# A hybrid decoder step on one core: constants in two groups, another order at the end of the samples' stage, and the decays squared on VectorE

## The chip, the core and the metric

The kernel runs on one core of a Trainium2 chip. The time is that of one execution on the device, in microseconds; each figure is the median over several runs of the same program. The engines are called as in the profile: PE (TensorE, the matrix multiplier), DVE (VectorE), ACT (ScalarE), POOL (GpSimd) and SP (SyncE, which issues most transfers). Each engine takes its own instructions in order and waits for others by semaphores.

## What is computed

One inference step of a decoder trunk with two layers, for a prompt of 512 tokens and, beside it, 8 samples of 8 tokens each (576 tokens in all, width 1024, float32). Layer 0 has a gated delta rule (4 heads of 128, a causal convolution of width 4, decays per head) beside a causal pooling, behind one input and one output projection. Layer 1 has a recurrent block (RG-LRU). Each mixer and each mixture of experts (16 experts, two per token) is followed by a layer norm. Cut to what the change touches:

```python
def delta_pool_mixer(x, ...):
    proj = x @ w_in
    qkv, z, b_raw, a_raw, u = jnp.split(proj, [c0, c1, c2, c3], axis=-1)
    qkv, conv_new = causal_conv(qkv, conv_hist, conv_w)
    ...
    o, s_new = gated_delta_rule(q, k, v, g, beta, s0)
    o = o * lax.rsqrt(jnp.mean(o * o, -1, keepdims=True) + RMS_EPS) * norm_w
    o = o * jax.nn.silu(z).reshape(bsz, T, A_HEADS, A_DV)
    ...
    y = jnp.concatenate([o_a, o_b], axis=-1) @ w_out

def rglru_mixer(x, ...):
    ...
    log_a = -C_GATE * r * jax.nn.softplus(-lam)
    a = jnp.exp(log_a)
    bt = jnp.sqrt(-jnp.expm1(2.0 * log_a)) * gi * xc
    # h_t = a_t * h_(t-1) + bt_t, then (h * y_branch) @ w_out
```

## The kernel before

Everything is written out by hand, one function per engine; the order on each engine is the order of the code, and counting semaphores tie the engines together. SBUF is one large tile `work` with many views whose lives follow one another. Tokens come in five tiles: four of 128 rows (the prompt) and one of 64 (the samples).

**The start.** SP issues the input (`x_prompt`, then `x_sample`, semaphore `x_in`), the router's weights and bias, the small columns `wab_in` of the input projection, five small transfers of histories and parameters (`hist_in`), and then the weights of the input projection, 1 MB at a time, into four slots `W0` (`w_in`). POOL makes the constants (`constants`, from L2410): first a memset of every one, then selects (`keep_where`, L2404) that cut `ident` and the masks out of them, then a few counters; its last instruction, the cast to `inv_cnt` (L2457), signals `consts_ready`. After it POOL issues two tiny transfers (`gpar`, for the gates). PE waits for `x_in` and `consts_ready` and transposes the tiles (`to_channels`, L609, eight per tile, two tiles in flight); ACT rounds each (`XT_HIGH`, L1248) and DVE makes the rest (`XT_LOW`, L1696). PE transposes the histories (L894 to L900), DVE prepares `wab` (L1912 to L1919), and PE runs its first product with it (L907, L908) and then twenty column blocks of the projection (`project`, L622, L623). DVE's `gates` (L1724 to L1740) come behind PE's first product, and its twelve convolutions behind the gates. From the fourth block on PE adds up squares with the constant `sum_col`.

**The end of the samples' stage.** The delta rule goes over four prompt chunks and then the samples. At its end the state of each head h is updated: PE multiplies (`state_update(h)`, L855, into banks 2 and 3 for even h, 5 and 6 for odd), DVE adds to the state (`new_states(h)`, L1886, eight instructions). Meanwhile the RMS norm of the outputs is applied: PE spreads the roots of head h (`root_spread(h)`, L863 and L864, banks 4 and 7; from the second on it waits for `rmsb_out`, that is for DVE to have read the one before), DVE multiplies (`normed(h)`, L1893 and L1894), POOL multiplies by the gate Z (L2533, `mix_a`). In between PE does early parts of the output projection (`out_part`, L964); the rest follows the last spread and reads `WO_HEADS`, 2 MB that SP issues behind the last state product. SP stores the new states (2 MB) behind `new_states(3)`, and then loads the first experts' weights.

**The second mixer.** Eight units m of 128 channels, in two halves of four. PE computes two gates per unit (L1223, L1224), ACT their sigmoids, then per unit the exponential (`XT[m]`, L1660, `lru_a`) and the tangent (`R_[m]`, L1663, `lru_t`), then the four square roots (L1667, each behind `lru_w`). Between them the square of the exponential is needed: POOL makes it (`squared`, L2618, `lru_a2`), DVE uses it (`root_input`, L2338, `lru_w`). DVE's `recurrence` (L2345 to L2355) and `result` (L2360, `mix_a`) follow the root of their unit. PE's output projection (L1014) takes unit after unit.

Behind each mixer a layer norm, the router and a loop over 16 experts (L1067, L1094) follow.

## Time and profile before

| what | us |
|---|---|
| median of 3 runs | 1407.63 |
| lowest, highest | 1405.70, 1408.05 |
| the profiled execution | 1408.48 |
| its span in the trace | 1406.70 |
| PE busy in the span | 1244.5 (88%) |
| DVE, ACT, POOL busy | 968.3 (69%), 730.8 (52%), 183.6 (13%) |
| mean granted clock of PE | 0.935 |

The times of the trace count from the start of the span; the execution is 1.78 us longer than it. PE's granted clock is given as a share of full speed (2.4 GHz). A busy share is a mean over stages with different limits: what a wait costs is read from its stage.

### The profile page before, as it was taken

What the parts mean: (1) busy time and instruction counts of PE and PEld (TensorE: products, weight loads), DVE (VectorE), ACT (ScalarE), POOL (GpSimd) and SP (SyncE); (2) the same over time, 40 slices, a digit from 0 to 9 for tenths busy, and PEclk for the clock granted to TensorE, in tenths of its full rate; (3) what the DMA queues carried; (4) which work ended last, traced back from release to release, by engine and by line L of the source; (5) the groups of instructions that cost most, each with busy time, mean ns of one, the idle gap of its engine ahead of it and who ended that gap; (6) DMA issues with size and microseconds to landing.
All of it is one profiled execution on the core that took longest, in us unless ns stands there. A gap on an engine that the chain in (4) does not pass through costs nothing.

```text
span 1406.7 us, 18287 instructions
## 1 busy us (share of the span) xinstructions
PE 1244.5 (88%) x6605; PEld 1008.7 (72%) x6605; DVE 968.3 (69%) x1441; ACT 730.8 (52%) x1011; POOL 183.6 (13%) x251
## 2 busy tenths in 40 slices
PE   4999988889999699999999289998987999999970
PEld 3988887777445588888888189964456888888860
DVE  3766355441534599999997553738656999999957
ACT  2543242221101388888886553256133888888844
POOL 4011442200300010000000300031001100000002
PEclk9999999996899699999999599999987999999995
DMA  6211051001242689999994822030545899999835
GB/s 204 61 61 60 1 191 33 1 1 53 86 183 90 233 331 403 417 417 405 419 408 147 255 85 91 1 150 1 198 173 220 340 408 420 411 417 403 350 109 198
DMA packets 63102, 296.61 MB, mean 211 GB/s; under 512 B 6624, under 2 KB 32969, under 8 KB 50752
## 3 DMA queue, kind: packets, MB, share of 16 engines
q1 hardware_dynamic: 51136, 252.78, 46.6%
q0 software_dynamic: 7296, 26.22, 5.2%
q10 hardware_dynamic: 4608, 16.78, 3.0%
q8 instruction: 40, 0.66, 0.2%
q14 instruction: 22, 0.18, 0.0%
HBM read 268.87 MB, written 26.89 MB: 210 GB/s over the span
## 4 chain that ended last, share of the span: by engine, by line
PE 83%; DVE 9%; ACT 2%; issue 2%; POOL 2%; DMA 2%; POOLq 0%; DVEq 0%; ACTq 0%
PE bank L1067 24%; PE bank L1094 12%; PE bank L977 6%; PE bank L622 5%; PE bank L623 4%; PE bank L648 4%; PE bank L650 4%; PE bank L964 2%; PE bank L1014 2%; PE bank L1057 2%; PE bank L1223 2%; PE bank L988 2%; PE bank L609 1%; PE bank L718 1%; PE bank L1085 1%
## 5 line engine op out<-in xcount | busy, mean ns | idle before, releaser
L1248 ACT ACTIVATE GU_HIGH<-work 128x1024 fp32r<-128x1024 f32 x256 | 270.2, 1060 | 63.3 <-PE bank L1067 59.2
L1067 PE MATMUL bank<-GU_HIGH,XGT_HIGH 128*128 128x512 f32 x512 | 203.0, 397 | 6.1 <-DVE XGT_LOW_B L2206 6.1
L2012 DVE TENSOR_TENSOR WGT_LOW<-work,GU_HIGH 128x1024 fp32r<-128x1024 f32 x128 | 155.5, 1223 | 13.4 <-ACT GU_HIGH L1248 5.5
L1248 ACT ACTIVATE WDN_HIGH<-work 128x1024 fp32r<-128x1024 f32 x128 | 135.4, 1063 | 44.2 <-PE bank L1094 44.2
L2012 DVE TENSOR_TENSOR WUP_LOW<-work,GU_HIGH 128x1024 fp32r<-128x1024 f32 x128 | 153.1, 1222 | 7.3 <-ACT GU_HIGH L1248 3.1
L2228 DVE TENSOR_TENSOR WDN_LOW<-work,WDN_HIGH 128x1024 fp32r<-128x1024 f32 x128 | 151.7, 1221 | 7.6 <-ACT WDN_HIGH L1248 3.7
L1067 PEld LDWEIGHTS bank<-GU_HIGH,XGT_HIGH 128*128 128x128 f32 x512 | 96.9, 189 | 26.0 <-DVE XGT_LOW_B L2206 6.9
L1248 ACT ACTIVATE work<-bank 128x512 f32<-128x512 f32 (+5 forms) x124 | 53.4, 469 | 115.1 <-PE bank L711 26.9
L1248 ACT ACTIVATE W_HIGH<-work 128x1024 fp32r<-128x1024 f32 x36 | 37.8, 1058 | 129.6 <-PE bank L623 80.0
L1067 PE MATMUL bank<-GU_HIGH,XGT_LOW_A 128*128 128x512 f32 x256 | 100.6, 393 | 0.0
L1067 PE MATMUL bank<-WGT_LOW,XGT_HIGH 128*128 128x512 f32 x256 | 100.2, 391 | 0.0
L1067 PE MATMUL bank<-GU_HIGH,XGT_LOW_B 128*128 128x512 f32 x256 | 100.0, 391 | 0.0
L1067 PE MATMUL bank<-WUP_LOW,XGT_HIGH 128*128 128x512 f32 x256 | 99.9, 390 | 0.0
L1094 PE MATMUL bank<-WDN_HIGH,HT_HIGH 128*128 128x512 f32 x240 | 96.4, 402 | 0.0
L1094 PE MATMUL bank<-WDN_HIGH,HT_LOW 128*128 128x512 f32 x240 | 93.7, 390 | 0.0
L1094 PE MATMUL bank<-WDN_LOW,HT_HIGH 128*128 128x512 f32 x240 | 93.5, 390 | 0.0
L977 PE MATMUL bank<-work,XT 128*128 128x512 f32 (+1 forms) x192 | 83.2, 593 | 0.0
L1463 ACT ACTIVATE lnw<-lnw 128x1 f32<-128x1 f32 (+1 forms) x10 | 2.0, 203 | 138.2 <-DVE lnw L2034 138.2
L977 PEld LDWEIGHTS bank<-work,XT 128*128 128x128 f32 (+1 forms) x192 | 32.8, 172 | 48.6 <-issue 48.0
L2558 POOL COPY idx_cur<-idx_all 128x1 int32 x28 | 7.0, 251 | 395.6 <-PE bank L1057 395.6
L1757 DVE SCALAR_TENSOR_TENSOR work<-work,par 128x512 f32<-128x512 f32 x120 | 56.9, 517 | 2.1
L1931 DVE TENSOR_TENSOR W_LOW<-work,W_HIGH 128x1024 fp32r<-128x1024 f32 x20 | 25.2, 1262 | 46.8 <-ACT W_HIGH L1248 46.6
(479 smaller groups left out, 2903.9 us busy)
## 6 DMA issues: line engine op xcount, KB each, us to landing
work<-in_moe_w_gate_dram SPq DMA_DIRECT2D x32, 2048.0 KB, 10.7
work<-in_moe_w_up_dram SPq DMA_DIRECT2D x32, 2048.0 KB, 10.5
work<-in_moe_w_down_dram SPq DMA_DIRECT2D x32, 2048.0 KB, 9.7
y_rows<-work ACTq DMA_DIRECT2D x32, 512.0 KB
work<-in_ab_w_in_dram SPq DMA_DIRECT2D x10, 1024.0 KB, 5.5
work<-in_c_w_in_dram SPq DMA_DIRECT2D x8, 1024.0 KB, 5.9
x_rows<-X SPq DMA_DIRECT2D x8, 512.0 KB, 2.6
work<-in_c_w_out_dram SPq DMA_DIRECT2D x1, 4096.0 KB, 15.7
```

Of the source, the lines that this page charges most:

```text
L622: mm(bank[c % 2][:, 0:TH], w[:, k, :], x[:, k, 0:TH], **ends)
L623: last = mm(bank[(3, 6)[c % 2]][:, 0:TH], w[:, k, :], x[:, k, TH:T], **ends)
L648: last = mm(bank[c % 3][:, 0:TH], w[:, k, :], x[:, k, 0:TH], **ends)
L650: last = mm(bank[(3, 6, 7)[c % 3]][:, 0:TH + 2], w[:, k, :], x[:, k, TH:T + 2], **ends)
L964: last = mm(bank[2 * (t % 2) + half][0:ROWS[t], :], XT[:, k, tile_cols(t)], (WO_A, WO_B)[l][k][:, 512 * half:512 * half + 512], start=(k = ...
L977: last = mm(bank[2 * (t % 2) + half][0:ROWS[t], :], XT[:, k, tile_cols(t)], (WO_A, WO_B)[l][k][:, 512 * half:512 * half + 512], start=(k = ...
L1067: last = mm(psum, x, w, start=(k == m == 0), stop=(k == KD - 1 and m == 2))
L1094: last = mm(bank[banks[half]][:, :], x[:, f, :], w[:, f, cols], start=(f == n == 0), stop=(f == 3 and n == 2))
L1248: return nc.scalar.activation(out, in_, ACT.Copy, scale=scale)
L1757: last = V.scalar_tensor_tensor(dst, src, w, dst, ALU.mult, ALU.add)
L2012: V.tensor_tensor(low[u][:, 2 * n:2 * n + 2, :], w[u][:, 2 * n:2 * n + 2, :], high, ALU.subtract)\
L2228: V.tensor_tensor(WDN_LOW[u][:, f, :], WDN[u][:, f, :], WDN_HIGH[:, f, :].bitcast(F32), ALU.subtract).then_inc(down_split, 1)
```

## The change

There are three parts. (1) At the start, POOL makes `ident` first and signals it by itself (`ident_ready`); then the constants and cleared buffers that are used early, signalled by `consts_ready`; then it issues the `gpar` transfers, and then makes the masks, signalled by `masks_ready`. PE's first transposes wait for `ident_ready`; DVE waits for `masks_ready` behind its gates, PE ahead of its first sum of squares. SP issues the first weights `W0[0]` ahead of the histories and the router's weights behind all weights of the projection. (2) At the end of the samples' stage, PE's `root_spread(2)` goes ahead of `state_update(3)`, and DVE's `new_states(3)` behind the last `normed`. (3) In the second mixer, DVE squares the decays inside `root_input`, and POOL's `squared` is gone.

```diff
--- before.py
+++ after.py
@@ -299,7 +299,7 @@
         state_out, y_out = sem("state_out"), sem("y_out")
         xrows_out, holds_ready, idx_ps, idx_ready = sem("xrows_out"), sem("holds_ready"), sem("idx_ps"), sem("idx_ready")
 
-        consts_ready = sem("consts_ready")
+        ident_ready, consts_ready, masks_ready = sem("ident_ready"), sem("consts_ready"), sem("masks_ready")
         xt_ps, xt_lo, xt_hi = sem("xt_ps"), sem("xt_lo"), sem("xt_hi")
         hist_ps, hist_out, ab_ps, rows_ready = sem("hist_ps"), sem("hist_out"), sem("ab_ps"), sem("rows_ready")
         wab_ready, gate_act, gate_dve = sem("wab_ready"), sem("gate_act"), sem("gate_dve")
@@ -520,10 +520,9 @@
                 sp.dma_start(to[0:TS, 4, :], x_sample.rearrange("s l d -> (s l) d")).then_inc(x_in, 16)
 
             load_x(X_IN)
-            sp.dma_start(rw[:, :, :], router_w.rearrange("(k p) e -> p k e", p=P)).then_inc(router_in, 16)
-            sp.dma_start(rbias[:, :], router_bias.partition_broadcast(P)).then_inc(router_in, 16)
             win = ab_w_in[0].rearrange("(k p) c -> p k c", p=P)
             sp.dma_start(wab_in, win[:, :, 2048:2056]).then_inc(wab_sem, 16)
+            sp.dma_start(W0[0], win[:, :, 0:256]).then_inc(w_in[0], 16)
             sp.dma_start(chist_rows[0:24, :], state_delta_conv[0].rearrange("s j c -> (s j) c")).then_inc(hist_in, 16)
             sp.dma_start(phist_rows[0:120, :], state_pool[0].rearrange("s j c -> (s j) c")).then_inc(hist_in, 16)
             sp.dma_start(par_rows[0:48, :], a_conv_w[0].rearrange("j (c p) -> (j c) p", p=P)).then_inc(hist_in, 16)
@@ -534,12 +533,15 @@
             for n, c in enumerate(cols):
                 if n >= 4:
                     sp.wait_ge(proj_ps, 2 * (n - 4) + 2)
-                sp.dma_start(W0[n % 4], win[:, :, c:c + 256]).then_inc(w_in[n % 4], 16)
+                if n:
+                    sp.dma_start(W0[n % 4], win[:, :, c:c + 256]).then_inc(w_in[n % 4], 16)
                 if n == 3:
                     sp.wait_ge(consts_ready, 1)
                     for l in range(2):
                         sp.dma_start(slot_list[l].rearrange("(p n) o -> p (n o)", p=P), zero_i[:, :])\
                           .then_inc(lists_zeroed, 16)
+            sp.dma_start(rw[:, :, :], router_w.rearrange("(k p) e -> p k e", p=P)).then_inc(router_in, 16)
+            sp.dma_start(rbias[:, :], router_bias.partition_broadcast(P)).then_inc(router_in, 16)
             sp.wait_ge(proj_ps, NPROJ)
             load_x(X)
             lnp(0, 0, ln_mix_g, ln_mix_b)
@@ -598,7 +600,7 @@
                         pe.wait_ge(norm_scaled if n == 2 else norm_done, (n - 1) * NT + t + 1)
                     elif t == 0:
                         pe.wait_ge(x_in, 32)
-                        pe.wait_ge(consts_ready, 1)
+                        pe.wait_ge(ident_ready, 1)
                     if n == 3 and t == 0:
                         pe.wait_ge(st1_out, 2)
                     if n * NT + t >= 2:
@@ -883,8 +885,8 @@
                 state_update(2)
                 root_spread(1)
                 out_part(0, 0, (NH + 3,), False, False)
+                root_spread(2)
                 state_update(3)
-                root_spread(2)
                 root_spread(3)
 
             def mixer0():
@@ -914,6 +916,7 @@
                         n = c - 3
                         pe.wait_ge(sq_done, n + 1)
                         if n == 0:
+                            pe.wait_ge(masks_ready, 1)
                             pe.wait_ge(rows_ready, 1)
                         ends = dict(start=(n == 0), stop=(n == 7))
                         mm(bank[4][0:8, :], sum_col[:, n, :], SQ[:, n % 2, 0:TP], **ends)
@@ -1903,9 +1906,9 @@
                 normed(0)
                 new_states(2)
                 normed(1)
-                new_states(3)
                 normed(2)
                 normed(3)
+                new_states(3)
 
             def mixer0():
                 dve.wait_ge(consts_ready, 1)
@@ -1948,6 +1951,7 @@
                 split_w(0)
                 split_w(1)
                 gates()
+                dve.wait_ge(masks_ready, 1)
                 dve.wait_ge(hist_out, 3)
                 for c in range(NCHUNK):
                     split_w(c + 2)
@@ -2333,8 +2337,10 @@
                         dve.wait_ge(ext1_zeroed, 1)
                     conv(m, EXT1[m % 3], lhistT[:, m, :], XC[:, m, :], KD, par[:, 32 + m:33 + m]).then_inc(conv_done, 1)
                 def root_input(m):
+                    dve.wait_ge(lru_a, m + 1)
+                    mine(V.tensor_tensor(TMP[:, m % 2, :], XT[:, m, :], XT[:, m, :], ALU.mult))
                     dve.wait_ge(lru_t, m + 1)
-                    dve.wait_ge(lru_a2, m + 1)
+                    mine.settle()
                     V.scalar_tensor_tensor(R_[:, m, :], TMP[:, m % 2, :], 1.0, R_[:, m, :], ALU.add, ALU.mult)\
                         .then_inc(lru_w, 1)
 
@@ -2405,23 +2411,32 @@
                                    channel_multiplier=mult))
 
             def constants():
-                for m, v in ((ident, 0.0), (ones, 1.0), (m_strict_bd, -1.0), (m_strict_off, -1.0), (m_strict_s, -1.0),
-                             (m_incl, 1.0), (m_incl_s, 1.0), (m_before, 1.0), (own_sample, 1.0), (ms_col, 0.0),
-                             (m_lower4, 1.0), (sel_gc, 0.0), (sel_row, 0.0), (sum_col, 0.0), (COL, 0.0), (scores, 0.5)):
+                do(G.memset(ident[:], 0.0))
+                G.affine_select(out=ident[:, :], in_=ident[:, :], compare_op=ALU.not_equal, fill=1.0, base=0,
+                                pattern=[[-1, P]], channel_multiplier=1).then_inc(ident_ready, 1)
+                mine(G.memset(wab, 0.0))
+                for m, v in ((ones, 1.0), (COL, 0.0), (scores, 0.5)):
                     mine(G.memset(m[:], v))
                 mine(G.memset(zero_i[:, :], 0))
                 mine(G.memset(norm_eps[:, 0:1], LN_EPS / ALPHA ** 2))
                 mine(G.memset(RT, 0.0))
                 mine(G.memset(keep, 1.0))
-                mine(G.memset(wab, 0.0))
                 mine(G.memset(U[:, :, 0:HIST], 0.0))
                 for buf in EXTB:
                     mine(G.memset(buf[:, 0:CONV - 1], 0.0))
+                do(G.iota(iota_i[:, :], pattern=[[1, 16]], base=1, channel_multiplier=0))
+                do(G.tensor_copy(inv_cnt[:, :], iota_i[:, :]))
+                mine(G.memset(keep[:, 0:TP].rearrange("p (c l) -> p c l", l=P)[:, :, 0], 0.0))
+                do(G.memset(keep[:, TP:T].rearrange("p (c l) -> p c l", l=LS)[:, :, 0], 0.0))
                 do(G.iota(tok_id[:, :], pattern=[[P, NT]], base=0, channel_multiplier=1))
-                mine(G.memset(keep[:, 0:TP].rearrange("p (c l) -> p c l", l=P)[:, :, 0], 0.0))
-                mine(G.memset(keep[:, TP:T].rearrange("p (c l) -> p c l", l=LS)[:, :, 0], 0.0))
-                keep_where(ident[:, :], [[-1, P]], 0, 1, 1.0, ALU.not_equal)
-
+                G.tensor_copy(tok_f[:, :], tok_id[:, :]).then_inc(consts_ready, 1)
+                for n, src in enumerate((a_dt_bias, a_log_decay)):
+                    pool.dma_start(gpar[32:36, n:n + 1], src.rearrange("o h -> h o")).then_inc(gates_in, 16)
+                for m, v in ((m_strict_bd, -1.0), (m_strict_off, -1.0), (m_strict_s, -1.0),
+                             (m_incl, 1.0), (m_incl_s, 1.0), (m_before, 1.0), (own_sample, 1.0), (ms_col, 0.0),
+                             (m_lower4, 1.0), (sel_gc, 0.0), (sel_row, 0.0), (sum_col, 0.0)):
+                    mine(G.memset(m[:], v))
+                mine.settle()
                 keep_where(m_strict_bd[:, :], [[-1, P]], -1, 1)
                 keep_where(m_strict_bd[:, :].rearrange("p (b c) -> p b c", b=2), [[-64, 2], [0, 64]], 0, 1)
                 keep_where(m_strict_bd[:, :].rearrange("p (b c) -> p b c", b=2), [[64, 2], [0, 64]], 63, -1)
@@ -2445,16 +2460,13 @@
                 keep_where(ms_col[:, :, :], [[1, NH], [-1, NH]], 0, 0, 1.0 / P, ALU.not_equal)
                 keep_where(m_lower4[:, :, :], [[1, 4], [-1, 4]], -1, 0)
                 keep_where(sum_col[:, :, :], [[1, 8], [-1, 8]], 0, 0, 1.0, ALU.not_equal)
-                do(G.tensor_copy(tok_f[:, :], tok_id[:, :]))
                 do(G.iota(slot_no[:, :].bitcast(I32), pattern=[[1, P]], base=0, channel_multiplier=0))
                 do(G.tensor_copy(slot_no[:, :], slot_no[:, :].bitcast(I32)))
                 do(G.iota(iota_i[:, :], pattern=[[1, NE]], base=0, channel_multiplier=0))
                 do(G.tensor_copy(iota16[:, :], iota_i[:, :]))
-                do(G.iota(iota_i[:, :], pattern=[[1, 16]], base=1, channel_multiplier=0))
                 mine(G.tensor_copy(before16[:, :], m_before[:, :]))
-                mine(G.tensor_copy(ones16[:, :], ones[:, :]))
                 mine.settle()
-                G.tensor_copy(inv_cnt[:, :], iota_i[:, :]).then_inc(consts_ready, 1)
+                G.tensor_copy(ones16[:, :], ones[:, :]).then_inc(masks_ready, 1)
 
             def tail(ready, n, buf, to, c, done):
 
@@ -2489,8 +2501,6 @@
                 st.end(G.tensor_tensor(to, QKV[:, 0:4, cols], egB[:, :, 0:n], ALU.mult), i, "qd")
 
             def mixer0():
-                for n, src in enumerate((a_dt_bias, a_log_decay)):
-                    pool.dma_start(gpar[32:36, n:n + 1], src.rearrange("o h -> h o")).then_inc(gates_in, 16)
                 for c in range(NCHUNK):
                     tail(proj_out, c + 1, EXTB[c % 3], tails, c, tail_done)
                 pool.wait_ge(conv_done, NCHUNK)
@@ -2611,19 +2621,9 @@
                     pool.wait_ge(lru_gates_done, 2 * m + 2)
                     G.tensor_tensor(GI[:, m, :], GI[:, m, :], XC[:, m, :], ALU.mult).then_inc(lru_x, 1)
 
-                def squared(m):
-                    pool.wait_ge(lru_a, m + 1)
-                    if m >= 2:
-                        pool.wait_ge(lru_w, m - 1)
-                    G.tensor_tensor(TMP[:, m % 2, :], XT[:, m, :], XT[:, m, :], ALU.mult).then_inc(lru_a2, 1)
-
                 half = KD // 2
                 for m in range(half):
                     gated_input(m)
-                for m in range(half):
-                    squared(m)
-                for m in range(half):
-                    squared(half + m)
 
             constants()
             mixer0()
```

What the order of the instructions becomes, at three places. On PE at the end of the samples' stage, from the third part of the early output projection (L964) on; L855 is a state update, L863 and L864 a spread. Before:

```order
L964 MATMUL bank<-work,XT 128x512 x2
L855 MATMUL bank<-work 128x512 x2
L863 MATMUL bank<-work,sel_row 128x512
L864 MATMUL bank<-work,sel_row 128x64
L863 MATMUL bank<-work,sel_row 128x512
L864 MATMUL bank<-work,sel_row 128x64
L964 MATMUL bank<-work,XT 128x512 x24
```

Now (the lines have moved by two or three):

```order
L967 MATMUL bank<-work,XT 128x512 x2
L865 MATMUL bank<-work,sel_row 128x512
L866 MATMUL bank<-work,sel_row 128x64
L857 MATMUL bank<-work 128x512 x2
L865 MATMUL bank<-work,sel_row 128x512
L866 MATMUL bank<-work,sel_row 128x64
L967 MATMUL bank<-work,XT 128x512 x24
```

The last state update has moved from ahead of the two last spreads to between them. On DVE at the same place, from the second `normed` (the pair that writes XT) on; the eight instructions with `egl` are a state update. Before:

```order
L1893 SCALAR_TENSOR_TENSOR XT<-work,par,bank 128x512
L1894 SCALAR_TENSOR_TENSOR XT<-work,par,bank 128x64
L1886 SCALAR_TENSOR_TENSOR work<-work,egl,bank 128x128 x8
L1893 SCALAR_TENSOR_TENSOR XT<-work,par,bank 128x512
L1894 SCALAR_TENSOR_TENSOR XT<-work,par,bank 128x64
L1893 SCALAR_TENSOR_TENSOR XT<-work,par,bank 128x512
L1894 SCALAR_TENSOR_TENSOR XT<-work,par,bank 128x64
L2025 SCALAR_TENSOR_TENSOR X<-X,bank 128x512 x2
```

Now:

```order
L1896 SCALAR_TENSOR_TENSOR XT<-work,par,bank 128x512
L1897 SCALAR_TENSOR_TENSOR XT<-work,par,bank 128x64
L1896 SCALAR_TENSOR_TENSOR XT<-work,par,bank 128x512
L1897 SCALAR_TENSOR_TENSOR XT<-work,par,bank 128x64
L1896 SCALAR_TENSOR_TENSOR XT<-work,par,bank 128x512
L1897 SCALAR_TENSOR_TENSOR XT<-work,par,bank 128x64
L1889 SCALAR_TENSOR_TENSOR work<-work,egl,bank 128x128 x8
L2029 SCALAR_TENSOR_TENSOR X<-X,bank 128x512 x2
```

The last state update has moved behind the three `normed`. On POOL at the start, the first instructions now; the twelve masks, their selects and the counters follow behind the last row:

```order
L2414 MEMSET ident 128x128
L2415 ISA
L2415 AFFINE_SELECT ident<-ident 128x128
L2417 MEMSET work 128x544
L2419 MEMSET ones 128x128
...
L2427 IOTA iota_i 128x16
L2428 CAST inv_cnt<-iota_i 128x16
...
L2432 CAST tok_f<-tok_id 128x5
L2434 DMA gpar<-in_a_dt_bias_dram 4x1
L2434 DMA gpar<-in_a_log_decay_dram 4x1
L2438 MEMSET m_strict_bd 128x128
```

Before, the select of `ident` stood behind all memsets, and the transfers of `gpar` behind all constants.

## Rows read from the trace of the kernel before

**Rows 1.** The page, part 4: the chain that ended last, by line.
```profile
PE bank L1067 24%; PE bank L1094 12%; PE bank L977 6%; PE bank L622 5%; PE bank L623 4%; PE bank L648 4%; PE bank L650 4%; PE bank L964 2%; PE bank L1014 2%; PE bank L1057 2%; PE bank L1223 2%; PE bank L988 2%; PE bank L609 1%; PE bank L718 1%; PE bank L1085 1%
```

**Rows 2.** Waits of PE, 0 to 60 us: total, times, longest.
```profile
PE bank L609 <- POOL inv_cnt L2457: 16.3, 1, 16.3
```

**Rows 3.** Timeline of POOL, 0 to 45 us: start, length, line, work.
```profile
5.69 0.29 POOL L2404 TENSOR_SCALAR_AFFINE_SELECT ident<-ident 128x128 f32<-128x128 f32 x1
...
20.08 0.55 POOL L2493 DMA_DIRECT2D gpar<-in_a_log_decay_dram  x1
```

**Rows 4.** Timeline of SP's queue, 0 to 60 us: its DMA issues.
```profile
0.82 0.47 SPq L519 DMA_DIRECT2D work<-in_x_prompt_dram  x1
1.35 0.58 SPq L520 DMA_DIRECT2D work<-in_x_sample_dram  x1
...
12.04 5.70 SPq L537 DMA_DIRECT2D work<-in_ab_w_in_dram  x4
```

**Rows 5.** DMA issues, 0 to 40 us: count, KB each, median us to landing.
```profile
work<-in_x_prompt_dram SPq DMA_DIRECT2D x1, 2048.0 KB, 8.9
work<-in_x_sample_dram SPq DMA_DIRECT2D x1, 256.0 KB, 9.9
```

**Rows 6.** The chain that ended last, 15 to 31 us: start, length, work.
```profile
16.31 3.55 PE bank L609 x16
...
21.07 1.30 DVE XT_LOW L1696 x2
...
22.42 1.11 PE bank L609 x8
...
28.41 0.48 PE bank L907
```

**Rows 7.** Timeline of DVE, 0 to 70 us: the last instruction of the gates.
```profile
46.62 0.82 DVE L1740 TENSOR_TENSOR work<-work 4x512 f32<-4x512 f32 x2
```

**Rows 8.** Windows: span, PE, PEld, DVE, ACT, POOL busy, PE clock, DMA, GB/s.
```profile
18.00:20.00 2.00, 1.85 (x10) 1.55 (x8) 0.52 (x1) 1.20 (x3) 0.70 (x1) 1.00 1.10 351
...
30.00:32.00 2.00, 2.00 (x10) 1.93 (x9) 1.58 (x2) 0.00 (x0) 0.00 (x0) 0.50 0.03 8
```

**Rows 9.** The chain that ended last, 362 to 392 us.
```profile
374.41 1.93 PE bank L855 x4
...
376.36 2.15 DVE work L1886 x8
378.51 0.66 DVE XT L1893
...
379.42 2.07 PE bank L863 x2
...
381.81 1.08 issue
```

**Rows 10.** Windows, columns as in rows 8, around 380 us.
```profile
376.00:378.00 2.00, 1.54 (x5) 0.66 (x4) 1.64 (x7) 0.00 (x0) 0.00 (x0) 1.00 0.15 27
...
387.00:388.00 1.00, 1.00 (x2) 0.34 (x1) 0.00 (x0) 0.00 (x0) 0.00 (x0) 0.50 1.15 349
```

**Rows 11.** Timeline of DVE in the second mixer (brackets: idle before).
```profile
950.53 0.75 DVE L2345 TENSOR_TENSOR work<-work 128x576 f32<-128x576 f32 x1
...
969.58 0.76 DVE L2338 SCALAR_TENSOR_TENSOR work<-work 128x576 f32<-128x576 f32 x1 [2.54 <-POOL work L2618]
```

**Rows 12.** Timelines of ACT and of POOL in the second mixer.
```profile
949.80 2.40 ACT L1667 ACTIVATE work<-work 128x576 f32<-128x576 f32 x4
...
948.22 1.53 POOL L2618 TENSOR_TENSOR work<-XT 128x576 f32<-128x576 f32 x1 [0.75 <-DVE work L2338]
```

**Rows 13.** Timelines of PE and of DVE at the second mixer's end.
```profile
990.62 3.60 PE L1014 MATMUL bank<-work,XT 128*128 128x512 f32 x8
...
988.59 0.76 DVE L2360 TENSOR_TENSOR XT<-work 128x576 f32<-128x576 f32 x1
```

**Rows 14.** DMA issues, 370 to 400 us, columns as in rows 5.
```profile
work<-in_ab_w_out_dram SPq DMA_DIRECT2D x1, 2048.0 KB, 8.6
```

## The prediction, made before the change was run

> **What bounds the kernel now.** I read the chain of work that ended last first: it lies mostly on TensorE (PE), and the two expert loops alone (L1067, L1094) are 36% of the span [rows 1]. The change touches neither loop. So it can only move the time at which PE gets through the stages around them, and I asked of each of its three places: does PE, or the chain that feeds it, wait there?
>
> At the start it does. PE has one long wait, 16.3 us, for `inv_cnt`, the last constant that POOL makes [rows 2]. `ident`, the only constant that the first transposes read, is ready at 5.98 and is made behind the memsets of all the others [rows 3]. The other thing that PE waits for is the input: `x_prompt` is issued at 0.82 and lands 8.9 us later, at 9.7; `x_sample` is issued at 1.35 and lands 9.9 us later, at 11.25 [rows 4, 5]. Behind the wait the chain goes tile by tile over PE, ACT and DVE, and PE starts its long run at 28.41 [rows 6].
>
> At the end of the samples' stage it does too. The chain goes from PE's state update (L855) to 2.15 us of DVE's state update (L1886), to DVE's `normed` (L1893), to PE's spread (L863, L864) [rows 9]. PE was through with the spread before at about 377.5 (376.34, and half of the 2.39 us, 379.42 to 381.81, that the same two lines take later at half clock) and starts the next at 379.42: 1.9 us of waiting for a `normed` of under 1 us that stands behind eight state instructions. The granted clock is 0.5 (1.2 GHz) from this pause on and still at 388; before it, it was 1.00 [rows 10].
>
> In the second mixer it does not. DVE waits for POOL's squares, 2.54 us in one place, yet its first recurrence (L2345, at 950.53) needs ACT's first square root, which starts at 949.80 and takes about 0.7 us [rows 11, 12]. The out-projection (L1014) has its last eight matmuls at 990.62, while DVE's last product ended at 989.35 [rows 13].
>
> **The start (-4.3 us).** `ident` becomes POOL's first work, a memset and 0.29 us of select, so ready before 2. PE then waits for `x_sample` alone and starts at 11.3 instead of 16.3: -5.0. The bounds: it cannot start before `x_prompt` is there, at 9.7 (-6.6). On the other side 1 MB of weights (`W0[0]`) now stands behind it in SP's queue where 72 KB of router weights stood; if the two shared the engines instead of following each other, 1 MB at the 351 GB/s of the weight stretch [rows 8] would cost 3.0 us (-2.0). I take -5.0, since `x_sample` stays second in the queue.
>
> PE gives a part back. The first sixteen transposes took 3.55 us (222 ns each), the eight of a later tile 1.11 (139 ns) [rows 6]: PE begins slow after its long idling. Tiles 2 and 3 may now come while it is still slow: 2 x 8 x 0.083 = 1.3 us. A tile starts only when DVE's 1.30 us for an earlier one are over (21.07 to 22.37, then PE at 22.42 [rows 6]), so part of it falls into PE's pauses. Bounds 0 and 1.3; I take half, 0.7. The granted clock reads 1.00 over these slow transposes [rows 8]; by that column there would be no such term, and the start would bring -5.0. The Trainium skill (TensorE: Matmul & The Clock Gate, What's actually happening) says that the default state is throttled and that activity releases it. That rule would hold the 0.7. The 222 ns speak against the column, and for them I keep the term. The long run began at 0.50 [rows 8]; I take the same again.
>
> What moves beside it. SP's queue: the first 1 MB of the four issued from 12.04 on [rows 4] goes ahead of the five small histories, the router weights (72 KB in two issues) behind all ten. PE reads the histories right behind the last tile, near 20.5; they were all issued by 12.0, and the 3.0 us of one more megabyte before them leaves 5 us. Bounds: 0, and 1 us if they land as late as `x_sample` did after its issue (12.0 + 9.9 = 21.9, less the pauses). I take 0. `W0[0]` itself is wanted by ACT near 21.5 and is now issued about 9 us sooner. POOL: `consts_ready` falls near 5; the two `gpar` transfers take the 4.5 us that they took (16.17 to 20.63), and and the masks take their part of the stretch from 5.98 to 16.17, 9.5 us, and 2 us of memsets [rows 2, 3]: they end near 21. DVE waits for `masks_ready` behind its gates, whose last instruction ended at 47.44 [rows 7] and now ends near 43: cost 0. Queued behind that wait are DVE's convolutions, and on PE the first sum of squares.
>
> **The samples' stage (-2.5 us).** From the end of the out-projection part at 374.41 PE now does: spread(2) 1.2, state update 1.93, spread(3) 1.2, then waits 1.08 for the last `normed`, as before [rows 9]. That ends at 379.8 instead of 382.89: -3.0. DVE has `normed(2)` during PE's state update, so spread(3) waits for nothing. The 3.0 are the 1.9 of waiting, and the 1.2 that the last spread took longer at half clock. But now 4.3 us of narrow products and the 1.08 pause stand in a row, and I expect the clock to fall there again, with a spread or the state update slowed. Bounds: the clock stays up and the 5.2 us at half clock from 382.9 to past 388 are saved too, -2.6; or it falls at once and stays low as long again, +2.6. I take 0.5 back.
>
> What is late next. The 2 MB `WO_HEADS` waits for the last state product, which comes 1.2 us later: issued at 377.6, landed 8.6 us later [rows 14] at 386.2. PE has the early part first, sixteen records at 3.60 us for eight [rows 13], so wants it at 387.0 at the soonest. Cost 0, with 0.8 us to spare. The state store goes out 3.5 us later and SP's first expert weights behind it; the loops that use them are 100 us away. DVE's moved 2.15 us lie where it waits for the out-projection.
>
> **The second mixer (0).** DVE takes over eight squares of 0.75 us (its product of this size [rows 11]). Per unit it needs 0.75 + 0.76 = 1.51 us, and ACT starts its roots at 949.80 in any case, behind its own table load. DVE begins when the first exponential is there, so its fourth root input ends near 949.3 and the recurrences begin with ACT's first root as now. What goes is DVE's idling. Were all of the squares to come on top, it would be 3.0 us per half, less 1.3 us of slack in the second [rows 13]; DVE idles 2.54 us ahead of its second half, so I take neither.
>
> **Sum.** -4.3 - 2.5 + 0 = -6.8 us. The profiled execution took 1408.48 us (1.78 around its span of 1406.70), which gives 1401.7. It is 0.85 above the median of the runs, 1407.63; against that, 1400.8 us.
>
> **The rivals.**
> *More comes of it* (chance 0.10): the clock does not fall in the samples' stage, or `x` lands by 10. Then -2.6 or -1.3 more: 1398.2 for the first. Against it: narrow products and a pause remain.
> *One term fails* (0.20): `x_sample` lands by 14.3 beside `W0[0]`, or the slow clock takes the samples' gain back. The sum is -3.8 to -4.3: 1403.6.
> *POOL stands in DVE's way* (0.06): the masks are now made while DVE splits the tiles. If they end 1.5 us later than 21, DVE's `WAB` instructions meet POOL's last ones (selects and casts, 0.29 us as the row of `ident` [rows 3]), and waiting for two of them costs 0.6 us on the path: 1401.4. The nearest row is a square on POOL beside DVE's work, 1.53 us [rows 12]. The Trainium skill (SBUF — State Buffer, Who interferes with whom) states an exclusive lock between these two engines, the later one waiting for the whole instruction.
> *The new wait decides* (0.03), the case on the other side: `masks_ready`. It costs one for one from the moment that the masks are later than DVE's gates, near 43; past 49.9 it has eaten the 6.8, and at 52 the time is 1409.7. For it: all convolutions and PE's fourth projection hang on it. Against: the 11.5 us of mask work would have to take 3.5 times as long.
> That the squares' move does nothing is part of the forecast itself.
>
> **How the numbers follow.** The forecast, both terms within a microsecond or so, has 0.61. About 0.2% (2.8 us) is what a measurement of this kernel can tell from no change; faster then means below 1404.8. The forecast, the first and the third rival lie there, and of the second three quarters: 0.61 + 0.10 + 0.06 + 0.15 = 0.92, of which I move 0.03 to "same" for terms that I have not seen: 0.89. Same 0.08, slower 0.03. The range takes in the first two rivals and what the runs themselves scatter (1405.7 to 1408.05): 1397.5 to 1404.5.
>
> **What would show it.** PE's first transpose at 11.3, released by the transfer and no longer by POOL; tiles 2 and 3 at 139 to 222 ns a transpose; the long run from 24.1 instead of 28.41; DVE never waiting for `masks_ready`. Then spread(3) without a wait, `WO_HEADS` not waited for. In the second mixer DVE's waits for POOL gone, and the distance from ACT's first root to PE's L1014 unchanged. Wrong would be: a later landing of `x_sample`, a wait on the histories at L894, or squares that show up in the chain.

## The result, and the profile after

The changed kernel takes 1398.51 us, the median of 4 runs (1397.54 to 1400.39), against 1407.84 us for the kernel before, run beside it (4 runs, 1405.70 to 1410.73). The ratio is 0.9935 with a 95% interval of 0.9914 to 0.9957, that is -9.2 us, between -12.1 and -6.1. It is faster, as forecast. The predicted 1400.8 us lies 2.3 us above the measured time, and the predicted gain of 6.8 us lies inside the interval, near its small end. The profiled execution took 1398.68 us with a span of 1396.3, so 2.4 us lie outside the span, where it was 1.8 before. Three executions in the experiments below took 1520, 1622 and 4796 us, one of them of the kernel before, and are left out of the ratios.

First the chain that ended last in the changed kernel, from 0 to 25 us (start, length, work), against [rows 6]:

```profile
1.35 9.68 DMA work<-in_x_sample_dram
...
11.07 1.98 PE bank L611 x8
...
15.61 3.69 PE bank L611 x16
...
24.12 0.48 PE bank L909
```

POOL is gone from it. PE's first transpose is released by the transfer of `x_sample`, as predicted: 11.07 instead of 16.31, so 5.24 us sooner. The long run (L909, L907 before) starts at 24.12 instead of 28.41, so 4.29 us sooner. The 0.95 us between the two numbers is what PE gave back in this profile: tiles 2 and 3 took 3.69 us for sixteen transposes, 230 ns each, where the kernel before had such a tile in 1.11 us. It is not the same in every profile, as the experiments show.

Next POOL's and SP's timelines of the changed kernel, against [rows 3, 4]:

```profile
4.95 0.75 POOL L2434 DMA_DIRECT2D gpar<-in_a_dt_bias_dram  x1
5.72 0.54 POOL L2434 DMA_DIRECT2D gpar<-in_a_log_decay_dram  x1
6.24 0.23 POOL L2438 MEMSET m_strict_bd<- 128x128 f32 x1
...
17.41 0.29 POOL L2469 CAST ones<-ones 128x128 f16<-128x128 f32 x1
```

```profile
1.98 0.57 SPq L524 DMA_DIRECT2D work<-in_ab_w_in_dram  x1
2.59 2.88 SPq L525 DMA_DIRECT2D work<-in_ab_w_in_dram  x1
5.52 4.66 SPq L526 DMA_DIRECT2D work<-in_state_delta_conv_dram  x1
...
11.71 5.22 SPq L537 DMA_DIRECT2D work<-in_ab_w_in_dram  x3
```

The masks are ready at 17.70, sooner than the 21 that I expected. They and their memsets take 11.5 us as estimated (6.24 to 17.70), but the two `gpar` issues take 1.3 us, not 4.5. PE's list of waits has no entry for the masks, and none for the histories. On SP's queue the issue of `W0[0]` (1 MB) holds the queue for 2.88 us and the next one for 4.66 us.

Then the end of the samples' stage in the chain of the changed kernel, against [rows 9]:

```profile
368.76 1.09 PE bank L865 x2
369.85 0.17 PE bank L866 x2
370.02 1.91 PE bank L857 x4
371.93 1.05 PE bank L865 x2
372.98 0.17 PE bank L866 x2
373.15 1.08 issue
374.23 22.54 PE bank L967 x48
396.76 3.43 PE bank L980 x8
```

DVE has left the chain. From the end of the early product to the output projection it is 5.47 us (368.76 to 374.23), where it was 8.48 (374.41 to 382.89): 3.01 us less, the predicted 3.0. The clock, windows of the changed kernel with the columns of [rows 8]:

```profile
375.00:377.00 2.00, 2.00 (x4) 0.97 (x3) 1.20 (x5) 0.00 (x0) 0.61 (x1) 0.50 1.02 418
387.00:388.00 1.00, 1.00 (x3) 0.38 (x2) 0.00 (x0) 0.00 (x0) 0.00 (x0) 1.00 0.93 197
```

It falls here again, as expected, but it comes back much sooner. Added up over windows of 1 us, it is at 0.50 for 3.4 us, from 374 to 378, where before it was at 0.50 for 10.2 us, from 378 to 389 [rows 10]. The L967 part (L964 before) runs without a pause, so `WO_HEADS` isn't waited for, and ends at 396.76 instead of 406.39: the gain has grown from 8.66 us at the projection's first product to 9.63, another 0.97 us. From the end of the early product to the end of this part it is 28.0 us instead of 32.0.

Last the second mixer, timelines of ACT, DVE and PE in the changed kernel (in brackets the idle time before), against [rows 11 to 13]:

```profile
939.67 2.40 ACT L1670 ACTIVATE work<-work 128x576 f32<-128x576 f32 x4
...
940.38 0.76 DVE L2351 TENSOR_TENSOR work<-work 128x576 f32<-128x576 f32 x1 [0.99 <-ACT work L1670]
...
958.04 0.76 DVE L2341 TENSOR_TENSOR work<-XT 128x576 f32<-128x576 f32 x1 [1.14 <-ACT XT L1663]
...
965.26 0.76 DVE L2351 TENSOR_TENSOR work<-work 128x576 f32<-128x576 f32 x1 [1.00 <-ACT work L1670]
...
956.24 24.20 PE L1017 MATMUL bank<-work,XT 128*128 128x512 f32 x56
```

DVE no longer waits for POOL. It waits for ACT, some 1 us in each half. From ACT's first root to the first record of the out-projection it is 16.57 us; before, the timelines have 949.80 and 966.48 for the two, 16.68 us. In this stage the squares' move is worth nothing, as predicted.

The spans differ by 10.4 us, the two executions by 9.8 (1408.48 and 1398.68), since 0.6 us more lie outside the span. The places above give 4.29 at the start, 3.01 in the samples' stage and 0.97 in the output projection, 8.3 together; the rest comes and goes on the way. Between the start and the samples' stage, where no wait that the change adds is felt, the gain grows from 4.29 to 5.65 us (374.41 against 368.76). It stands at 9.63 us behind the first output projection, at 7.96 at the last product of the first expert loop (773.14 against 765.18), at 10.24 at the second mixer's out-projection. What differs is the clock: added up over windows of 1 us as far as 1340 us, near the end of the last expert loop, PE's granted clock is at 0.50 for 143.4 us before and for 136.5 us after (over the whole spans 182.5 and 176.0). Half of the 6.9 us, up to 3.4, is what that can be worth. As many as 6.8 us of these 6.9 are what the samples' stage and its output projection differ by (10.2 against 3.4 us), which is where the change acts; elsewhere the two kernels gain and lose about as much.

### The profile page after: what moved, and what is told of

It is laid out like the page before. It is cut to its first block, busy times and chain, and to the rows that moved or that the text cites. A ratio compares the mean times of both kernels' runs of the same rounds, so it can differ in the third digit from the quotient of the medians.

```text
span 1396.3 us, 18281 instructions
## 1 busy us (share of the span) xinstructions
PE 1243.7 (89%) x6605; PEld 1009.9 (72%) x6605; DVE 972.4 (70%) x1449; ACT 730.6 (52%) x1011; POOL 172.2 (12%) x243
## 4 chain that ended last, share of the span: by engine, by line
PE 83%; DVE 9%; ACT 3%; issue 2%; DMA 2%; SPq 0%; POOL 0%; POOLq 0%; DVEq 0%; ACTq 0%
PE bank L1070 25%; PE bank L1097 13%; PE bank L980 6%; PE bank L624 5%; PE bank L625 4%; PE bank L650 4%; PE bank L652 4%; PE bank L967 2%; PE bank L1017 2%; PE bank L1060 2%; PE bank L1226 2%; PE bank L991 2%; PE bank L611 1%; PE bank L720 1%; PE bank L1088 1%
## 5 line engine op out<-in xcount | busy, mean ns | idle before, releaser
L1070 PEld LDWEIGHTS bank<-GU_HIGH,XGT_LOW_A 128*128 128x128 f32 x256 | 48.9, 191 | 10.5
## 6 DMA issues: line engine op xcount, KB each, us to landing
work<-in_moe_w_gate_dram SPq DMA_DIRECT2D x32, 2048.0 KB, 10.4
work<-in_moe_w_up_dram SPq DMA_DIRECT2D x32, 2048.0 KB, 10.2
y_rows<-work ACTq DMA_DIRECT2D x32, 512.0 KB, 10.4
```

The lines of the kernel that those rows point to most:

```text
L1070: last = mm(psum, x, w, start=(k == m == 0), stop=(k == KD - 1 and m == 2))
```

## The experiments

Ratios are to the kernel before, run on the same chip in the same set; microseconds are the ratio times its median of 1407.

**The parts alone.** Four kernels. `e1_start` and `e3_squares` are the change's hunks for the start and for the second mixer alone. `e2_samples` and `e4_dve_order` are

```diff
on DVE, e2_samples and e4_dve_order:
-                new_states(3)
                 normed(2)
                 normed(3)
+                new_states(3)
on PE, e2_samples alone:
+                root_spread(2)
                 state_update(3)
-                root_spread(2)
                 root_spread(3)
```

> Part 1 alone: the split constants, their order on POOL and the order of SP's first DMAs; the samples' stage and the second mixer as in the kernel before. Theory A (the three parts add up as the prediction priced them, and what the full change gained beyond 6.8 us is PE's clock, which falls elsewhere when the same work lies elsewhere): the first transpose at 11.1 instead of 16.3, the long run of matmuls of L907 from 24.1 instead of 28.4, and that 4.3 us kept to the end but for the clock: -4.3 us, from -7.7 to -0.9 if one more or one fewer stretch of 3.4 us is at 1.2 GHz at the end. Theory B (the start itself earns more later than its 4.3 us, for instance because the first mixer's transfers or DVE run further ahead): -7 us or more, with stalls that are gone in places other than the start, at an unchanged granted clock. If A holds, the difference of the spans minus half of the difference of the time at 1.2 GHz is the same 4.3 us plus what the stages' own waits differ.

> Part 2 alone: in the samples' stage PE's spread of the root of head group 2 ahead of the state update of 3, and DVE's new_states(3) behind the two normed steps; the rest as in the kernel before. Theory A: from the last L964 product of the stage to the first product of the output projection the stretch is 3.0 us shorter, as in the full change (from 8.5 to 5.5 us), and the total goes by -3.0, from -6.4 to +0.4 with a stretch of 3.4 us at 1.2 GHz more or fewer. Theory B (the reordering earns only when the earlier start comes with it): under 1.5 us gained at this place.

> Part 3 alone: DVE squares the decays of the second mixer itself. Theory A (DVE waited for ACT's roots anyway, and the four squares of a half, 3.0 us of DVE's time, go into that wait): 0, within 1 us, and from ACT's first root to the first product of the output projection 16.7 to 16.9 us as before. Theory B (POOL's squares stood in the way, since POOL and DVE share a port or since DVE's wait for two engines came through late): -1 to -2.5 us, seen between the same two points. Theory C (DVE becomes the one that is late): +1 to +3 us, seen there too.

> Only DVE's half of part 2: new_states(3) behind normed(2) and normed(3), with PE's order as before (state_update(3), then root_spread(2) and (3)). Theory A (what ended the stage late was DVE, which normed the last two groups behind a new_states that nobody there needed: L1886 took 2.15 us in the chain): most of the 3.0 us, -2.0 to -3.0, comes from DVE's half alone. Theory B (the halves need each other, since the spread of group 2 waited behind state_update(3) on PE, 1.93 us of L855 in the chain): at most -1.1 at this place, as one half takes away only its own part of the chain and the other takes its place.

| kernel | ratio, 95% interval | us |
|---|---|---|
| start alone | 0.9956 [0.9939, 0.9972] | -6.2 |
| samples' stage alone | 0.9976 [0.9960, 0.9993] | -3.4 |
| squares alone | 0.9995 [0.9981, 1.0008] | -0.7 |
| DVE's half of the samples' stage | 0.9998 [0.9980, 1.0016] | -0.3 |

The three parts add up to -10.3 us against the -9.2 of the whole. Within the intervals, which are some 2 us to either side for each, none needs another. The intervals of the start (-8.6 to -3.9) and of the samples' stage (-5.6 to -1.0) hold the 4.3 and the 2.0 to 3.0 that the traces show at their places. Nothing in the runs asks for theory B at the start: the long run begins at 24.19, as in the whole change. The squares alone give 16.74 us from ACT's first root to the first record of the out-projection (948.67 to 965.41), as theory A had it, and 44.33 us to the projection's second block (993.00), against 44.26 before (949.80 to 994.06). They also show which part the 0.6 us outside the span come with: 2.4 us lie outside it with the squares on DVE, 1.7 to 1.8 in the kernel before, in `e1_start` and in `e2_samples`. Why is open, the more so as `e6_twice`, which has squares on DVE too, has 2.0.

The samples' stage needs the clock of its spread told apart from its order. Kernel `e1_start` has the old order there. Its chain:

```profile
369.07 1.92 PE bank L857 x4
...
371.02 2.16 DVE work L1889 x8
373.18 0.66 DVE XT L1896
...
374.08 1.12 PE bank L865 x2
...
375.44 1.08 issue
376.52 23.55 PE bank L967 x48
```

It is the chain of [rows 9] link by link, except that the spread (L865 here, L863 there) takes 1.12 us and not 2.07, since the clock falls a little later. The stretch is 7.45 us (369.07 to 376.52). `e2_samples`, with both halves of the new order and the old start, takes 5.46 us (371.36 to 376.82), as theory A had it. So as far as the output projection, and with the spread near full speed, the reordering is worth 7.45 - 5.47 = 1.98 us, and the other 1.03 of the 3.01 are that spread's clock.

With DVE's half alone the stretch was 6.53 us (374.53 to 381.06), 0.92 less than 7.45; expected were at least 2.0 (theory A) or at most 1.1 (theory B). So B holds as far as the output projection. To the end of the projection it is another matter, as the table below shows.

**PE's half alone, the whole once more, the old queue, and the start given back.**

```diff
 after_again: the changed kernel, unaltered
 e9_pe_order (kernel before): root_spread(2) ahead of state_update(3); DVE's order as before
 e5_old_queue (start alone): SP issues rw, rbias ahead of wab_in, W0[0] behind the histories
 e8_masks_gate (changed kernel):
-                        pe.wait_ge(ident_ready, 1)
+                        pe.wait_ge(masks_ready, 1)
```

> The changed kernel once more, unaltered. Theory A (the parts earn 4.3 us at the start and 2.0 to 3.0 in the samples' stage, which is what the same points of the traces show at equal clock, and the rest of what was measured is where TensorE's time at 1.2 GHz happens to fall): the ratio comes out between 0.9935 and 0.9960, -5.6 to -9.2 us, and the profile again differs from the sum of the parts by half of the difference of the time at 1.2 GHz. Theory B (something lasting beyond the parts): again 0.9935 or below.

> Only PE's half of part 2: root_spread(2) ahead of state_update(3), DVE's order as before; the complement of the run with DVE's half, which took 6.53 us from the end of the last early L964 product to the output projection, where the kernel before took 8.48 (of this 0.95 because L863 ran at 1.2 GHz) and both halves take 5.46. Theory A (the halves split the 2.0 us evenly, each in its own link of the chain: PE's half hides the 1.93 us of state_update(3) under DVE's norm): 6.5 us, and the total by -1.0 but for the clock. Theory B (PE's half alone gives nothing, since DVE's norm of group 3 still ends last behind new_states): 7.5 us, no gain at this place.

> Part 1 without its change of SP's queue: the split constants as in the change, but SP issues the router's weights behind the input and the first block of the first mixer's weights behind the histories, as before; parts 2 and 3 left out. It is to be compared with part 1 alone, -6.2 us, and tells whether the queue's new order matters. Theory A (the clock of the start is the input's landing and ident alone): the first transpose at 11.1, the long run of L907 from 24.1, W0 of block 0 landed by 22 and nobody waiting for it; the time as part 1 alone within the scatter. Theory B (the queue's order carries part of the gain): PE waits for w_in behind the gate's columns, the first mixer's first matmuls start later by as much, up to 3 us.

> The changed kernel, but its first transpose waits for the masks (the end of all of POOL's constants, at 17.7 us) instead of for ident; the rest unaltered. It gives the start back and keeps all other moves. Theory A (each microsecond of the first transpose is one of the end): the first transpose at 17.7 instead of 11.1, the end later by 6.6 us than the changed kernel's, -1.5 to -4 us against the kernel before. Theory B (the start is worth less than it looks, since later stages wait for transfers or other engines that don't move with it): later by less than 4 us. Theory C (more than it looks): later by 8 us or more.

| kernel | ratio, 95% interval | us |
|---|---|---|
| the changed kernel again | 0.9948 [0.9932, 0.9965] | -7.3 |
| PE's half of the samples' stage | 1.0002 [0.9990, 1.0014] | +0.3 |
| start alone, old queue | 0.9964 [0.9950, 0.9978] | -5.1 |
| changed, first transpose behind the masks | 0.9997 [0.9985, 1.0009] | -0.4 |

The whole change came to -7.3 us this time, in the middle of what theory A gave. The -6.8 of the sum lies in both intervals, so the times alone show nothing lasting beyond the priced parts, and don't exclude 2 or 3 us of it. Its profile has the first transpose at 10.58, tiles 2 and 3 at full speed and the long run from 22.75, and again 28.0 us from the end of the early product to the end of the L967 part.

With PE's half alone, the chain from the same point on (374.22, the end of the early product):

```profile
374.22 1.09 PE bank L863 x2
...
375.47 1.93 PE bank L855 x4
...
377.42 2.16 DVE work L1886 x8
379.58 0.66 DVE XT L1893
...
380.48 2.07 PE bank L863 x2
...
382.87 1.08 issue
383.95 22.31 PE bank L964 x48
```

It is 9.73 us, 1.25 longer than the 8.48 before at the same clock (both have the spread at 2.07). That is worse than either theory had it (6.5 and 7.5 us, or a microsecond more with the slow spread). DVE still does its state instructions first, and these now wait for a state update that comes behind the spread. So neither half gives the 1.98: DVE's alone gains 0.92, PE's alone loses 1.25. The total of `e9_pe_order` shows no gain either.

The count up to the output projection leaves out what the clock does behind it. Measured from the same point, the end of the early product, in all profiles (us; the last column adds up windows of 1 us as far as the projection's part L964 or L967 goes):

| order | to the output projection | to the end of its part | clock at 0.50 |
|---|---|---|---|
| old, the kernel before | 8.48 | 32.0 | 10.2 |
| old, `e1_start`, `e3_squares`, `e5_old_queue` | 7.40 to 7.63 | 31.0 each | 6.8 each |
| PE's half alone | 9.73 | 32.0 | 6.8 |
| DVE's half alone | 6.53 | 28.8 | 3.4 |
| both halves, six profiles | 5.46 to 5.47 | 28.0 each | 3.4 each |

The six are the changed kernel twice, `e2_samples`, `e8_masks_gate`, and `e6_twice` and `e10_first_tile` from further below. So the shorter time at 1.2 GHz comes with the new order each time, whatever the start did: the stage is worth 3.0 us against three profiles of the old order and 4.0 against the kernel before's. Counted this way, DVE's half alone gives 2.2 of the 3.0, theory A's share after all, while its total (-0.3, from -2.8 to +2.3) can't tell.

The old queue gives the start's gain as well. W0[0] is then issued at SP's usual place behind the histories, the first transpose comes at 10.49, and PE waits for no weights. The two intervals overlap largely: the new order of the queue is worth nothing that can be measured. What does differ is the pace of the tiles, PE's timeline of this kernel:

```profile
10.49 3.33 PE L609 MATMUL bank<-ident,work 128*128 128x128 f32 x16 [10.49 <-DMA work<-in_x_sample_dram]
15.04 1.09 PE L609 MATMUL bank<-ident,work 128*128 128x128 f32 x8 [1.22 <-DVE XT_LOW L1697]
16.38 1.09 PE L609 MATMUL bank<-ident,work 128*128 128x128 f32 x8 [0.25 <-DVE XT_LOW L1697]
```

Tiles 2 and 3 are at full speed here, and the long run begins at 22.62, though the transposes began only 0.58 us sooner than in the changed kernel. It isn't the queue that does it: the changed kernel's second profile has the same. Nor is it the change. `e2_samples` and `e4_dve_order` have the old start, instruction for instruction, and their transposes begin at the same 16.23. Tile 2 in the second profile of the changed kernel, in `e2_samples`, and tiles 2 and 3 in `e4_dve_order`:

```profile
15.12 1.09 PE L611 MATMUL bank<-ident,work 128*128 128x128 f32 x8 [0.87 <-DVE XT_LOW L1699]
...
20.75 1.09 PE L609 MATMUL bank<-ident,work 128*128 128x128 f32 x8 [1.21 <-DVE XT_LOW L1696]
...
20.75 3.67 PE L609 MATMUL bank<-ident,work 128*128 128x128 f32 x16 [0.87 <-DVE XT_LOW L1696]
```

From the first transpose to the long run it is 12.1 us in the kernel before, in `e2_samples`, here, and 12.2 in the changed kernel's second profile; it is 13.0 to 13.4 in `e3_squares`, `e4_dve_order` and `e9_pe_order`, which have the old start, as in the changed kernel's first profile and `e1_start`. So the term that I took as half of 1.3 us is scatter of both kernels, not a price of the change. The long run begins at 28.33 to 29.61 in five profiles with the old start, and at 22.62 to 24.19 in six with the new one (without the two whose input is split and the one that waits for the masks).

Waiting for the masks moves the first transpose to 17.85 and the long run to 31.23, 7.1 us later than in the changed kernel, and costs 0.9997 - 0.9948, 6.9 us at the end, give or take some 3 us by the two intervals. At the end of the L967 part it is 7.3 us (404.11 against 396.76), so as far as there each microsecond of the start is kept; the end agrees with that (theory A) but wouldn't exclude 8. Against the kernel before, A's -1.5 to -4 us was missed: it is -0.4 (-2.1 to +1.3). The long run is 2.8 us later than before's, which eats up the 3 to 4 us of the samples' stage. It also shows what the split itself is for: with one semaphore for all constants in this order of POOL's, 17.7 us would still stand where 11.07 does.

**What is left to gain, and how much cover the squares have.** Four variants of the changed kernel; the last has both edits.

```diff
 e6_twice: each square of root_input(m) issued twice
 e7_no_pause, in out_and_route(0):
-                    pe.wait_ge(rmsb_out, NH)
                     e_dve.wait(pe, 0, "s2")
 e10_first_tile, on SP and on PE:
+            sp.dma_start(X_IN[:, 0, :], x_prompt[0, 0:P, :]).then_inc(x_first, 16)
+            sp.dma_start(X_IN[:, 1:4, :], x_prompt[0, P:4 * P, :]...).then_inc(x_in, 16)
...
                     elif t == 0:
+                        pe.wait_ge(x_first, 16)
                         pe.wait_ge(ident_ready, 1)
+                    elif t == 1:
                         pe.wait_ge(x_in, 32)
```

> The changed kernel with each of DVE's eight squares in the second mixer done twice: 8 x 0.75 = 6.0 us more on DVE between ACT's roots and the output projection, 3.0 in each half. Theory A (the four squares of a half are hidden, since DVE waits 1.0 to 1.1 us for ACT in each half and once between them, and PE has 1.45 us left behind DVE's last product; so about 4.5 us of cover is left beyond what the change used): from ACT's first root to the first product of the output projection 18.0 to 19.5 us instead of 16.7, the total +1.5, up to +3. Theory B (DVE is far from the end here): 16.7, +0. Theory C (the single squares were at the edge already): +6, the stretch 22 to 23.

> The changed kernel without PE's wait for rmsb_out in front of the early part of the output projection's second tile; PE then waits there for e_dve and, ahead of the late part, for mix_a. What ended the pause of 1.08 us in the changed kernel is not named in its chain. Theory A (it is this wait, that is DVE's L1896 and L1897 on head group 3): the pause goes, the out-projection begins behind L866, and the total goes by -1.1. Theory B (DVE's other products, for which e_dve waits, or the late part's wait for mix_a end as late as that): the pause stays or comes back 32 products of L967 on, total 0.

> The changed kernel, but the first 128 rows of the prompt come by a DMA and a semaphore of their own (0.5 MB), and PE's first eight transposes wait for these alone; the others wait for the other rows and the sample. Theory A (what bounds the start now is the landing of 2.25 MB, 9.7 us behind its issue, and after it a pace of 4.5 us per tile): the first transpose at 5 to 7 us, the second tile's at 10.0 to 11.5, the long run of L909 from 19.5 to 20.5 instead of 24.1, the total by -4. Theory B (the next thing is late: W0 of block 0 or wab, issued behind the input, or the histories): PE waits for w_in or wab_ready, the run begins at 21 or later and the total goes by -1 to -3. Theory C (the tiles' pace is lost where it is gained, since PE waits for the second tile): the run begins at 23 or later, total 0 to -1.

> The two edits together: the first tile by its own DMA, and no wait for rmsb_out ahead of the early part. Theory A: they add, -4 and -1.1: about -5 us against the changed kernel, -12 to -14 against the one before. Theory B (one of them gives nothing): as the better one alone.

| kernel | ratio, 95% interval | us |
|---|---|---|
| squares twice | 0.9960 [0.9942, 0.9978] | -5.6 |
| no pause | 0.9937 [0.9916, 0.9957] | -8.9 |
| first tile by itself | 0.9923 [0.9899, 0.9948] | -10.8 |
| both edits | 0.9914 [0.9888, 0.9940] | -12.1 |

Squares twice, timelines of ACT and PE:

```profile
939.02 1.83 ACT L1670 ACTIVATE work<-work 128x576 f32<-128x576 f32 x3
941.95 0.68 ACT L1670 ACTIVATE work<-work 128x576 f32<-128x576 f32 x1 [1.10 <-DVE work L2346]
...
957.94 13.90 PE L1017 MATMUL bank<-work,XT 128*128 128x512 f32 x32
972.63 10.57 PE L1017 MATMUL bank<-work,XT 128*128 128x512 f32 x24 [0.79 <-DVE XT L2368]
```

Root to out-projection is 18.92 us instead of 16.57, inside theory A's 18.0 to 19.5, and now ACT's fourth root waits for DVE, and PE for DVE's product. To the second block of the projection it is 47.57 us (to 986.59) against 44.15 (to 983.82), 3.4 us for 6.0 us of added work, about a microsecond of which is the clock. So some 2.6 to 3.6 us of the added work were still covered, less than the 4.5 that I expected; the single squares of the change are not at the edge. The total, 1.7 us above the changed kernel's -7.3, is near theory A's +1.5 too.

Without the wait for `rmsb_out` the chain has no pause:

```profile
376.62 1.53 PE bank L865 x2
378.16 0.32 PE bank L866 x2
378.48 23.50 PE bank L967 x48
```

The 1.08 us are gone at their place, so that wait was what ended them. But they aren't gained. The spread now takes 1.53 us instead of 1.05, and the part behind it 23.50 instead of 22.54: the clock falls before the spread is over and is at 0.50 for 6.8 us instead of 3.4. From the end of the early product to the end of the part it is 28.5 us (373.46 to 401.98), 0.5 longer than the 28.0 with the pause. In the total the kernel is at -8.9 against -7.3 and -9.2 of the changed kernel, which can't tell either way.

The first tile by itself, PE's timeline:

```profile
4.47 1.97 PE L615 MATMUL bank<-ident,work 128*128 128x128 f32 x8 [4.47 <-DMA work<-in_x_prompt_dram]
10.42 3.67 PE L615 MATMUL bank<-ident,work 128*128 128x128 f32 x16 [3.98 <-DMA work<-in_x_sample_dram]
14.95 1.09 PE L615 MATMUL bank<-ident,work 128*128 128x128 f32 x8 [0.86 <-DVE XT_LOW L1703]
```

The first 0.5 MB lands 3.6 us after its issue, and the long run begins at 20.88 instead of 24.12, 3.2 us sooner: between the 4 of theory A and the 1 to 3 of B. A took the first tile to save its whole pace of 4.5 us. But the second tile can't start before the rest of the input is there, so PE stands idle 3.98 us between them. No wait for weights is new. Against the changed kernel's second profile, whose long run began at 22.75, it is only 1.9 us. In the total it is 3.5 us ahead of the changed kernel as measured in the set before (0.9948 against 0.9923), and both edits together 4.8 us (0.9914); the medians of these two, 1396.6 and 1396.8 us, are alike. In the profile with both edits the long run begins at 20.83, and the stretch from the early product to the end of the projection's part, without the pause, again takes 28.5 us instead of 28.0. So the places give the first tile 1.9 to 3.2 us and the dropped wait half a microsecond of loss. The version with both edits beats the kernel before clearly. Against the changed kernel the intervals still overlap, so that advantage rests on the places in the trace, which show it for the first tile alone.

## Why the prediction was right

**The start, -4.3: right, 4.29 us.** `x_sample` alone set it. The transfer landed 9.68 us after its issue, against 9.9, so neither bound came true: `W0[0]` behind it didn't slow it (over the profiles with the whole input in two transfers it is 9.0 to 9.9 us with the old queue, 9.2 to 9.7 with the new). The first transpose was 0.2 us sooner than forecast, and PE gave back 0.95 us where I took 0.7. That the two make 4.29 is luck. The 5.0 was sound and came out as 5.2 to 5.8; the 0.7 was taken for a price of the change, and the runs show slow tiles with the old start about as often. In the changed kernel's second profile nothing is given back, and the start brings 5.66 us against the kernel before's profile. In the first profile the slow transposes of tiles 2 and 3 are what was given back, while the granted clock reads 1.00 over them, as it does over the first transposes before [rows 8]: the window 18 to 20 us holds the last of them and reads

```profile
18.00:20.00 2.00, 1.29 (x7) 0.89 (x5) 1.19 (x2) 1.38 (x4) 0.00 (x0) 1.00 1.10 350
```

The durations and not the column were right. In `e1_start` the column reads 1.00 from 8 to 44 us, while the products of its long run take 0.24 us each until 27.07 and 0.13 us after. The Trainium skill (TensorE: Matmul & The Clock Gate, What's actually happening), by which the engine starts throttled until it has been active, agrees with the 230 ns; no run here shows more of that rule.

**What moved beside it.** The masks' time was missed by 3.3 us because I took a gap of 4.5 us on POOL (16.17 to 20.63) for the cost of two `gpar` issues. In both kernels these take 1.3 us, and the rest of the gap was POOL standing idle 3.14 us ahead of them. It changed nothing: DVE asks for the masks only behind its gates, whose end moved from 47.44 to 43.48. SP's queue cost 0, as said, though for a reason other than mine: two issues hold the queue for 7.5 us together (2.88 and 4.66) while the input passes, and with the old order two others held it for nearly as long (3.15 and 4.26 us in the kernel before, 2.91 and 3.84 in `e5_old_queue`), though these were the issues of smaller transfers.

**The samples' stage, -2.5: too small.** The mechanism was right in each link, and the 3.0 came out as 3.01: 1.98 from the order and 1.03 from the spread that is no longer slow. The step that failed is the "0.5 back" for the clock. It fell as expected, on the first products of the output projection, but it rose again within them, after 3.4 us instead of 10.2, and 0.97 us more came in where 0.5 were to be lost. The sum for this stage is -4.0 in this profile, inside the bounds of 2.6 around -3.0. Against the three other profiles of the old order, whose clock was low for 6.8 us, it is -3.0; all six profiles of the new order have the 3.4. The first rival (2.6 us more, if the clock stays up) is thus partly true. Why the clock comes back sooner with the new order is not shown.

**The second mixer, 0: right.** 16.57 us against 16.68. DVE's idling went, nothing else. The sum took 1.78 us outside the span as given, though; with the squares on DVE it is 2.4, a loss of 0.6 us that the forecast doesn't have and whose cause is open.

**The other rivals.** DVE's splits of the first tile (14.27 to 15.57) run while POOL makes masks (6.24 to 17.70) and take 1.30 us, as in [rows 6], where POOL was through. They are no test of the lock between the two engines that the Trainium skill states: the same section (SBUF — State Buffer, Who interferes with whom) exempts a DVE instruction with at most one input in SBUF, and these read one of their two from a bank (PSUM), with which the unchanged 1.30 us agree. The `WAB` instructions, for which I feared it, came at 22.5, when the masks were done, so no run here tries it on them. The new wait for `masks_ready`, the case on the other side, is 25.8 us from deciding anything (17.70 against 43.48).

**The sum.** -6.8 against -9.2 (-12.1 to -6.1) in the first comparison and -7.3 (-9.6 to -4.9) in the second. By the places, the start brings 4.3 to 5.7 us and the samples' stage 3.0 to 4.0, less the 0.6 outside the span: 6.7 to 9.1, against the 7.3 and 9.2 measured. The profiled executions differ by 9.8. Of the time at 1.2 GHz that the changed kernel saves, the part in the samples' stage came with the new order in every profile. The rest is scatter, as two things show. `e2_samples` is the kernel before up to the end of the early product, and gets there at 371.36 where that one does at 374.41, 3 us sooner without any edit. And the kernel before by itself scatters: in 29 runs it took 1405.06 to 1408.65 us in 22, at a mean granted clock of 0.933 to 0.938, and 1410.84 to 1412.13 us in the other 7, at 0.930 to 0.932. The same program, without any edit, moves by 5 us with its clock. What stays open is whether the earlier start, too, makes a better clock likelier; the two comparisons of the changed kernel, 1.9 us apart, can't tell. That the sum lay within 2.4 us of the first and 0.5 of the second owes something to two misses that go against each other, the loss outside the span and the samples' stage being worth more.

## What to carry to other kernels

A wait on one semaphore for many things costs as much as the last of them: ask what the first consumer reads, make that first, and ask next what will be late in its place (here the input, which could in turn be split). Where two engines hand work back and forth, an instruction that nobody waits for belongs behind those that somebody does, on both engines at once: up to the output projection PE's half alone cost 1.25 us, both together gained 1.98. A gain below 0.3% is read at its place in the trace, since the total of one and the same kernel moves by more; and the place ends where the clock is up again, not where the pause ends. Dropping a pause of 1.08 us made the stage 0.5 us longer, and the reordering brought a microsecond or two beyond what its own links show. One profile of each kernel is not enough for that: the same start, from the same 16.23 us on, took 12.1 us in one and 13.4 in another.
